# Twelve expert blocks ahead of the loop, a search that starts after half a head, and comparisons on ScalarE

## The reference: what is computed

```python
q = (xb @ w_q).reshape(PEER_BLOCK, PEER_HEADS, 2, PEER_HALF)
s = jnp.einsum('thpd,hpnd->thpn', q, sub_keys)        # 8 heads, 2 halves, 128 keys each
s_top, i_top = lax.top_k(s, PEER_TOPK)                # 16 of 128, for each half
cand = s_top[:, :, 0, :, None] + s_top[:, :, 1, None, :]
best, pos = lax.top_k(cand.reshape(...), PEER_TOPK)   # 16 of 256 pairs
expert = jnp.take_along_axis(cand_idx, pos, axis=-1)
g = jax.nn.softmax(best, axis=-1)
act = jax.nn.gelu(jnp.einsum('td,thkd->thk', xb, u[expert]))
return jnp.einsum('thk,thkd->td', (g * act), v[expert])
...
mem_kv = _rmsnorm(mem, norm_mem) @ w_mem_kv
```

## Time and profile before

| | |
|---|---|
| median of 3 runs | 1432.37 us (1431.96 to 1432.41) |
| profiled execution, its own time | 1430.41 us |
| its span in the trace | 1428.7 us |
| mean granted TensorE clock | 0.999 of full speed |
| PE busy | 1402.6 us (98% of the span) |
| DVE busy | 992.6 us (69%) |
| ACT busy | 738.5 us (52%) |
| POOL busy | 183.2 us (13%) |

### The profile page before, as it was taken

How to read it: one execution, slowest core, us unless ns; L and a number is a source line. 1 busy time by engine, 2 the same in 40 slices (tenths; PEclk the granted TensorE clock), 3 DMA queues, 4 the chain that set the end, 5 groups by cost and what they waited for, 6 DMA issues and landing times.

```text
span 1428.7 us, 22032 instructions
## 1 busy us (share of the span) xinstructions
PE 1402.6 (98%) x7854; PEld 1210.0 (85%) x7854; DVE 992.6 (69%) x1748; ACT 738.5 (52%) x1118; POOL 183.2 (13%) x165
## 2 busy tenths in 40 slices
PE   9999999998999999999999999999999999999998
PEld 9888887797788888888888888888889899888886
DVE  6688389899766666666666666666678564665665
ACT  5655311378555555555555555555555734465433
POOL 0072134699000000000000000000000100000000
PEclk9999999999999999999999999999999999999999
DMA  6553530310555555555555555555544432333532
GB/s 212 178 186 109 198 126 31 131 47 16 185 189 189 189 189 191 190 190 186 188 187 190 190 191 190 185 191 185 177 177 170 155 130 107 135 131 147 204 150 103
DMA packets 57510, 229.14 MB, mean 160 GB/s; under 512 B 6752, under 2 KB 9072, under 8 KB 48752
## 3 DMA queue, kind: packets, MB, share of 16 engines
q1 hardware_dynamic: 56992, 228.19, 46.6%
q10 hardware_dynamic: 464, 0.20, 0.1%
HBM read 226.27 MB, written 2.10 MB: 160 GB/s over the span
## 4 chain that ended last, share of the span: by engine, by line
PE 88%; DVE 7%; ACT 2%; issue 1%; POOL 1%; DMA 1%; DVEq 0%; POOLq 0%; ACTq 0%
PE ps L2343 23%; PE ps L2116 17%; PE ps L2332 13%; PE ps L2082 8%; PE ps L2330 8%; PE ps L2318 4%; PE ps L2038 3%; PE ps L2328 2%; PE ps L2157 2%; PE ps L2295 1%; DVE lo L1402 1%; PE ps L1996 1%; DMA raw<-in_v_t 1%; PE ps L2460 1%; PE ps L2453 1%
## 5 line engine op out<-in xcount | busy, mean ns | idle before, releaser
L1641 DVE TENSOR_TENSOR lo<-raw,hi 128x1024 fp32r<-128x1024 f32 x234 | 286.0, 1222 | 61.7 <-ACT hi L1049 61.7
L2332 PE MATMUL ps<-x,hi 128*128 128x512 f32 x826 | 296.8, 398 | 0.0
L1049 ACT ACTIVATE hi<-raw 128x1024 fp32r<-128x1024 f32 x234 | 245.9, 1051 | 0.0
L2330 PE MATMUL ps<-x,lo 128*128 128x256 f32 x944 | 245.6, 281 | 0.0
L2116 PE MATMUL ps<-hi,x 128*128 128x512 f32 x704 | 224.8, 393 | 0.6 <-DVE lo L1402 0.4
L1402 DVE TENSOR_TENSOR lo<-raw,hi 128x2048 fp32r<-128x2048 f32 x60 | 140.1, 2336 | 72.8 <-ACT hi L894 72.8
L2330 PEld LDWEIGHTS ps<-x,lo 128*128 128x128 f32 x944 | 178.5, 189 | 9.2
L2332 PEld LDWEIGHTS ps<-x,hi 128*128 128x128 f32 x826 | 155.2, 188 | 33.1
L1104 ACT ACTIVATE oi<-ps 128x256 f32<-128x256 f32 x118 | 45.4, 385 | 229.6 <-PE ps L2332 228.5
L2116 PEld LDWEIGHTS ps<-hi,x 128*128 128x128 f32 x704 | 132.2, 188 | 28.9 <-issue 1.5
L2343 PE MATMUL ps<-hi,wh 128*128 128x512 f32 x484 | 150.4, 392 | 1.3 <-DVE wl L1655 1.1
(11 more groups left out here) (402 smaller groups left out, 2271.4 us busy)
## 6 DMA issues: line engine op xcount, KB each, us to landing
raw<-in_v_t SPq DMA_DIRECT2D x128, 512.0 KB, 3.5
raw<-in_u_t SPq DMA_DIRECT2D x126, 512.0 KB, 3.5
raw<-in_pieces SPq DMA_DIRECT2D x61, 1024.0 KB, 4.8
ring<-in_peer_w_q SPq DMA_DIRECT2D x4, 2048.0 KB, 8.1
big<-in_up SPq DMA_DIRECT2D x4, 2048.0 KB, 8.6
ring<-in_w_mem_kv SPq DMA_DIRECT2D x1, 2048.0 KB, 7.7
resid<-in_x SPq DMA_DIRECT2D x2, 512.0 KB, 4.4
raw<-in_pieces SPq DMA_DIRECT2D x2, 512.0 KB, 7.7
```

Of the source, the lines that this page charges most:

```text
L1049: act.activation(hi[:, which, par], raw[:, which, par], ACT.Copy).then_inc(hi_done[which], 1)
L1641: dve.tensor_tensor(lo[:, which, par], raw[:, which, par], hi[:, which, par].bitcast(F32), ALU.subtract).then_inc(lo_done[which], 1)
L2330: pe.matmul(first, u_lo[:, par, c], xh[:, c], start=False, stop=False)
L2332: ins = pe.matmul(both, u_hi[:, par, c], x2[:, :, c], start=False, stop=(c == KC - 1))
```

## The change

Three things are changed together. First, `AHEAD` goes from 10 to 12, and the chunks are spread anew: 20 before the pick transposes, 12 while the picks are copied (as before), and one after each of the 64 half groups. The two more gelu results go to a new tile `h_keys`, which lies in the memory of `wh` and `wl`, one of the three homes of the rounded product; so the first four blocks use the two others in turn, and the wait for `v_mm` in front of the third and fourth is new or one longer.

Second, in rounds 0 and 1 PE makes queries and scores half a head at a time, with one step of memory between, and DVE begins to search as soon as the first half of a head is there. The second head of a round is searched whole. Rounds 2 and 3 go a head at a time in place of two.

Third, in rounds 0 and 1 ACT makes the comparisons of places: for each of the two places, 16 activations Abs(i - place) of 64 columns and one Relu(1 - x) of 1024. They stand in ACT's stream behind the evacuations of rounds 1 to 3.

```diff
-AHEAD = 10
-BY_HEAD = 2
-CHUNKS_BEFORE_PICKS = 32
-CHUNKS_BEFORE_BUILD = 44
-BLOCKS_BEFORE_PICKS = 4
+AHEAD = 12
+BY_HALF = 2
+ACT_ROUNDS = 2
+CHUNKS_BEFORE_PICKS = 20
+CHUNKS_BEFORE_BUILD = 32
+BLOCKS_BEFORE_PICKS = 2
...
-        h_ahead = [h_first[:, b] for b in range(2)] + [h_raw[:, b] for b in range(AHEAD - 2)]
+        h_ahead = [h_first[:, 0], h_first[:, 1], h_keys[:, 0], h_keys[:, 1]] + [h_raw[:, b] for b in range(AHEAD - 4)]
...
-            return ((wh[:], wl[:]), (wh_odd, wl_odd), (wh_third, wl_third))[(j + KEY_SHIFT) % 3 if j < AHEAD - 1 else 0]
+            homes = ((wh[:], wl[:]), (wh_odd, wl_odd), (wh_third, wl_third))
+            return homes[1 + j % 2] if j < 4 else homes[(j + KEY_SHIFT) % 3 if j < AHEAD - 1 else 0]
...
-                    pool.wait_ge(matched, 2 * r + k + 1)
+                    if r < ACT_ROUNDS:
+                        pool.wait_ge(logf_then_act_matched, 1 + 2 * r + k + 1)
+                    else:
+                        pool.wait_ge(matched, 2 * (r - ACT_ROUNDS) + k + 1)
...
+            def compare_places(r, k):
+
+                kept = pick[:, r % 2, (1, 0)[k]]
+                act.wait_ge(fgate_then_places_done, 1 + r + 1)
+                for i in range(TOP):
+                    act.activation(kept[:, :, :, i], places_of[:, r % 2, (1, 0)[k]], ACT.Abs, scale=-1.0, bias=iota[:, i:i + 1]).then_inc(act_step, 1)
+                steps[0] += TOP
+                act.wait_ge(act_step, steps[0])
+                flat_kept = kept.rearrange("p c k i -> p (c k i)")
+                act.activation(flat_kept, flat_kept, ACT.Relu, scale=-1.0, bias=1.0).then_inc(logf_then_act_matched, 1)
+
+            for r in range(BY_HALF):
+                for h in range(2):
+                    for a in range(2):
+                        out_half(r, h, a)
+                        out_scores(8 * r + 4 * h + 2 * a, 8 * r + 4 * h + 2 * a + 2)
+            compare_places(0, 0)
             out_query(2, 0)
+            out_scores(16, 18)
+            compare_places(0, 1)
             out_query(2, 1)
-            out_scores(8, 10)
+            out_scores(18, 20)
+            compare_places(1, 0)
             out_query(3, 0)
+            out_scores(20, 22)
+            compare_places(1, 1)
             out_query(3, 1)
-            out_scores(10, 12)
+            out_scores(22, 24)
...
-                if j >= 3:
-                    act.wait_ge(v_mm, j - 2 if j < AHEAD - 1 else j)
+                if j >= 2:
+                    act.wait_ge(v_mm, j - 1 if j < 4 else j - 2 if j < AHEAD - 1 else j)
...
+                for h in range(2):
+                    if r < BY_HALF and h == 0:
+                        for a in range(2):
+                            dve.wait_ge(sub_out, scores_until(r, h, a))
+                            search(halves[a::4])
+                    else:
                         dve.wait_ge(sub_out, scores_until(r, h))
                         search(halves[2 * h:2 * h + 2] + halves[4 + 2 * h:4 + 2 * h + 2])
-                        search_pairs((h,))
-                else:
-                    dve.wait_ge(sub_out, scores_until(r))
-                    search(halves)
-                    search_pairs((0, 1))
+                    search_pairs((h,))
...
+                if r < ACT_ROUNDS:
+                    dve.tensor_tensor(place[:, 1], p1, p4, ALU.subtract).then_inc(fgate_then_places_done, 1)
+                    continue
...
+            for r in range(BY_HALF):
+                for h in range(2):
+                    for a in range(2):
+                        k = 4 * r + 2 * h + a
+                        g = half_features(r, h, a)
+                        memory(19 + k, 20 + k)
+                        if k == 0:
+                            pe.wait_ge(cols_then_mem_loaded, 96)
+                        key_scores(2 * k, 2 * k + 2, g)
+            features("wq2", actT, (0,))
             memory(27, 29)
-            key_scores(8, 10, "wq21")
-            features("wq3", actT, (0, 1))
+            key_scores(16, 18, "wq20")
+            features("wq2", actT, (1,))
             memory(29, 31)
-            key_scores(10, 12, "wq31")
-            memory(31, MEM_STEPS)
+            key_scores(18, 20, "wq21")
+            features("wq3", actT, (0,))
+            key_scores(20, 22, "wq30")
+            features("wq3", actT, (1,))
+            memory(31, 32)
+            key_scores(22, 24, "wq31")
+            memory(32, MEM_STEPS)
```

More of the change, by code:

```diff
@@ L132, in build @@
         mhalf = sb("mhalf", [P, 16])
+        h_keys, = lease(("h_keys", [P, 2, T], F32))
         wh = sb("wh", [P, T], F32R)
@@ L347, in build @@
                    "hgate0", "hgate1", "ggate0", "ggate1",
-                   "mk0", "wq00", "wq01", "wq10", "wq11", "wq20", "wq21", "wq30", "wq31", "mk1", "mv0", "mv1"]
+                   "mk0", "wq00", "wq00b", "wq01", "wq01b", "wq10", "wq10b", "wq11", "wq11b", "wq20", "wq21", "wq30", "wq31", "mk1", "mv0", "mv1"]
         group_no = {g: i for i, g in enumerate(groups1)}
+        half_bank = {f"wq{r}{h}{b}": (4 * r + 2 * h + k) % 3 for r in range(BY_HALF) for h in range(2) for k, b in enumerate(("", "b"))}
         mem_bank = {"mk0": 2, "mk1": 3, "mv0": 2, "mv1": 3}
@@ L376, in build @@
         posf = takeP(3, NT, 2 * TOP)
-        place = takeP(2, NT * 2, TOP)
+        places_of = takeP(2, 2, NT * 2, TOP)
         pick = takeP(2, 2, NT * 2, TOP, TOP)
@@ L932, in _ @@
             split_2nd_after("glow")
-            act.wait_ge(fgate_done, 1)
-            act.activation(feat(gF[:, 0:4]), feat(gF[:, 0:4]), ACT.Ln).then_inc(logf_done, 1)
+            act.wait_ge(fgate_then_places_done, 1)
+            act.activation(feat(gF[:, 0:4]), feat(gF[:, 0:4]), ACT.Ln).then_inc(logf_then_act_matched, 1)
             act.wait_ge(gate_mm, 1)
@@ L1439, in _ @@
             wait_marked()
-            dve.tensor_scalar(kF[:, 0:4], gF[:, 0:4], -1.0, 1.0, ALU.mult, ALU.add).then_inc(fgate_done, 1)
+            dve.tensor_scalar(kF[:, 0:4], gF[:, 0:4], -1.0, 1.0, ALU.mult, ALU.add).then_inc(fgate_then_places_done, 1)
             piece_split_lo("gqk1", "glow", "hi0", "hi1")
@@ L1596, in _ @@
                 link(dve.tensor_copy(posf, posi))
+                place = places_of[:, r % 2]
+                if r >= 2:
+                    dve.wait_ge(logf_then_act_matched, 1 + 2 * (r - 2) + 2)
                 p1, p4, p16 = (posf[:, k].rearrange("p n (h k) -> p (n h) k", h=2) for k in range(3))
@@ L2262, in key_scores, with half_features @@
                     ins.then_inc(sub_done, 1)
-            features("wq0", actT, (0,))
-            memory(19, 21)
-            pe.wait_ge(cols_then_mem_loaded, 96)
-            key_scores(0, 2, "wq00")
-            features("wq0", actT, (1,))
-            memory(21, 23)
-            key_scores(2, 4, "wq01")
-            features("wq1", actT, (0,))
-            memory(23, 25)
-            key_scores(4, 6, "wq10")
-            features("wq1", actT, (1,))
-            memory(25, 27)
-            key_scores(6, 8, "wq11")
-            features("wq2", actT, (0, 1))
+            def half_features(r, h, a):
+                need(f"wq{r}")
+                g, f0 = f"wq{r}{h}" + ("b" if a else ""), (2 * h + a) * P
+                bank_free(g)
+                for c in range(KC):
+                    ins = pe.matmul(ps[:, gbank(g), 0:T], tile_view(f"wq{r}")[:, c, f0:f0 + P], actT[:, c], start=(c == 0), stop=(c == KC - 1))
+                ins.then_inc(group_done, 1)
+                return g
+            for r in range(BY_HALF):
[8 more added lines that the diff above has]
+            features("wq2", actT, (0,))
             memory(27, 29)
-            key_scores(8, 10, "wq21")
-            features("wq3", actT, (0, 1))
+            key_scores(16, 18, "wq20")
+            features("wq2", actT, (1,))
             memory(29, 31)
-            key_scores(10, 12, "wq31")
-            memory(31, MEM_STEPS)
+            key_scores(18, 20, "wq21")
[5 more added lines that the diff above has]
+            memory(32, MEM_STEPS)
             def ahead(first, last):
```

39 lines of the change are left out of this document (17 added, 22 removed).

## The result

The changed kernel takes 1440.14 us (median of 5, 1438.60 to 1441.01), the kernel before 1432.37 (median of 5, 1430.00 to 1432.56). The ratio is 1.0058, with a 95% interval of 1.0047 to 1.0068: slower, by 7.8 (0.6%, and clear of the spread), where 1.4 less was forecast, and outside the range given.

The account below looks back on a forecast made before the run. PE was taken to bound the kernel (88% of the chain), with DVE setting the time of the picks. Terms -2.8 + 1.1 + 3.5 + 1.9 - 5.1 = -1.4 gave a median of 1431.0, range 1428.0 to 1435.0.

Parts of the forecast that it names:

- Scores by the half head: PE's queries and scores: 4.63 a half, 0.21 more than now, 1.7 for eight; memory product ends 3.0 later.
- Search: DVE's search for the picks: starts sooner, DVE alone the bound from round 2 on, picks 2.8 earlier.
- Comparisons on ACT: ACT's comparisons of places in rounds 0 and 1: a pass takes 5.2 and is hidden.
- The rival with long passes: ACT's comparisons at 8 a pass delay evacuations and POOL's last pick: total +5.2, 1437.6; chance 0.10.
- Build: Half groups after the picks: a new wait of 1.1, then 64 half groups with a chunk, 3.5 more.
- The new wait: At the build's start, PE's first chunk waits for block 2's gelu behind the first evacuation: 1.1.
- Behind the build: PE's next pass waits 2.5 for the rounding of `actT`, no longer covered by the build: 1.9 more.
- Two more blocks: Keys ahead of the loop: two loop bodies fall away, 11.1, two key blocks cost 6.0; 5.1 saved.
- The clock falls: PE's longer waits halve its clock, so chunks after the picks take 5 longer: +3.6, 1436.0; chance 0.07.

Follow-up runs that it names:

- e1: The changed kernel with POOL's product with the keys and three wide sums left out in rounds 0 and 1: 1432.48 us, ratio to before 1.0006.
- e8: The kernel before with twelve blocks ahead, keeping 32 chunks before the picks and 44 before the build: 1428.49 us, ratio to before 0.9981.
- e3: The changed kernel with ACT's rounding of actT cut into four pieces, most of them ahead of PE's last chunk: 1436.84 us, ratio to before 1.0037.
- e2: The changed kernel with unread matmuls in PE's waits, 26 before the picks' transposes and 10 before the first pass: 1435.52 us, ratio to before 1.0027.
- e11: The changed kernel with 32 chunks before the picks, 44 before the build and four gelus before the picks: 1431.15 us, ratio to before 0.9996.
- e6: The kernel before with only the new plan of blocks (twelve ahead, 20 and 32 chunks), search and comparisons unchanged: 1436.46 us, ratio to before 1.0032.

## Why the prediction was wrong

**Scores by the half head: right.** 4.64 a half where 4.63 was forecast; the memory product ends 86.05 after the start, forecast 85.5.

**Search: the step that failed.** It said that from round 2 on "DVE alone is the bound" and priced its 16.3 a round as if nobody could hold it, so picks 2.8 earlier. Without POOL's passes they came 2.3 earlier (e1), so the reading of the search was right within 0.5; with them they came 2.4 later. By the rows, 5.1 of the missing 5.2 is 2.1 in the pair sums of round 1, 0.8 in those of round 2 (0.65 and 1.06, where 0.44 is the row of before), and 2.2 in the comparison of round 2. The prediction looked at POOL only for when it is done, and at ACT's passes only for their length. That the passes would let POOL start at a time of ACT's choosing, and no longer right behind DVE's own comparison, was in the order of the code and was not weighed. DVE's rows of before show no stall to warn of it, since there the two engines missed each other, once by 0.36. But POOL's do: its product takes 3.27 where it starts beside DVE's second comparison (243.72 and 263.95 in the earlier trace rows) and 2.35 to 2.37 where it starts behind its own sums, so the same line stood there at two durations:

```profile
208.78 2.37 POOL L796 TENSOR_TENSOR big<-big 128x1024 f32<-128x1024 f32 x1
```

**Comparisons on ACT: right.** 5.1 a pass, forecast 5.2, hidden. The rival with long passes is out.

**Build: right in one part, long in another.** The new wait was 1.05 (1.1). The build with its last chunk (284.57 to 370.83) was 4.9 longer than the 81.3 of before; forecast 4.6. Half groups with a chunk follow each other at 1.325 (288.08 to 370.23 for 62). In e8, 16 more of them cost 1.4, 0.09 each, where the prediction has 0.125.

**Behind the build: the mechanism right, the size short.** The wait was 2.37, forecast 2.5, and e3 shows that it was the rounding. From the build's last work to the first product (370.83 to 377.60) it cost 3.2 more than the 3.57 of before; forecast 1.9. At full clock it is 1.7 (2.37 and e2's 2.89, less 3.57), and the clock is the other 1.5.

**Two more blocks: right.** -11.2 and +6.2, forecast -11.1 and +6.0.

**The clock falls** had 0.07 and a clock term of 5, all of it behind the picks (its +3.6 is that term less the forecast's 1.4). It came, with 2.2 behind the picks and 1.5 behind the build, 3.7 in all. In this kernel the first part followed from the collisions, which made PE's wait 6.27: with e1's wait of 1.55 it did not come. But it takes the plan too, which took twelve chunks out of that wait: with them back (e11) there is no wait, and with the plan alone (e6) the clock falls without any collision. In the prediction's sum the chance of a fall behind a wait of 2.4 was too low, since three of the five profiles with it show one (below).

Sum: -1.4 forecast, +5.2 at the picks (4.7 of it POOL's, by e1, and 0.5 that the search gained less than read), +2.2 and +1.5 of clock, +0.3 in small terms: 7.8.

## What to carry to other kernels

When a step moves to a third engine, look at what that engine now releases and when: an instruction of POOL's that used to start right behind DVE's own may start in the middle of DVE's chain, and an instruction of DVE's of the kinds above may then wait for the end of it. Price it as one POOL instruction for each meeting, and look in the profile for the same line at two durations. Work that fills PE's wait before a late result is worth more than the same work later, since it costs nothing there and keeps the clock: taking 12 chunks from ahead of the picks into the build, where they seemed cheap, is most of what this change lost, together with the two waits (1.05 and 2.37) that the last chunks and the gelus then made.

## What the runs showed of the hardware

The stall is whole: 2.40 for a pair sum of 0.22 when POOL's product of 2.35 began 0.1 earlier; 1.64 for both when it had begun 1.0 earlier. That is so for POOL's TENSOR_TENSOR. In the build it is POOL that pays: its 64 TENSOR_SCALAR of the kernel before take from 0.79 to 2.09, while DVE's 32 wide comparisons beside them take 1.21 to 1.23, all of them, even one that by the records began 0.28 behind POOL's. Why that one did not wait stays open.

```profile
275.26 2.09 POOL L810 TENSOR_SCALAR ring<-oi,ring 128x128 f32<-128x128 f32 x1
```

```profile
275.54 1.22 DVE L1628 TENSOR_TENSOR ring<-oi,ring 128x1024 f32<-128x1024 f32 x1
```

The clock, in eleven profiles with a wait of PE before the picks' transposes: behind waits of 0.47, 0.64, 1.15, 1.27, 1.35 and 1.55 (the first two with matmuls that nobody reads ahead of them) the way to the build took 5.89 or 5.90. Behind 4.09, 6.20, 6.27, 7.39 and 7.87 the same work took 7.48, 8.55, 8.07, 7.83 and 7.41, with granted clocks of 0.78, 0.68 and 0.72 in the first three: between 1.5 and 2.7 more, without order by the length of the wait. Behind the wait of 2.37 at the first pass it fell in three profiles (4.40, 4.41, 4.30 to the first product) and not in two (2.90, 2.85), in kernels that are the same at that place. The Trainium skill (TensorE: Matmul & The Clock Gate, What's actually happening) has it that idleness halves the clock; the trace agrees, and which of the waits of 2.37 does so stays open. So does the start of the query matmuls, 2.4 apart from one execution to another in identical code.
